# Prompt heads of a decoder step: the values of two heads together, and sums over later key blocks made on GpSimd

## The reference

```python
z = jnp.einsum('bqhd,bkhd->bhqk', q, k) * (SB_HEAD_DIM ** -0.5)
z = z + bias[None, :, None, None]
causal = (k_pos[None, :] < q_pos[:, None])[None, None]
log_stay = jnp.where(causal, jax.nn.log_sigmoid(-z), 0.0)
between = lax.cumsum(log_stay, axis=3, reverse=True) - log_stay
weight = jnp.where(causal, jnp.exp(jax.nn.log_sigmoid(z) + between), 0.0)
return jnp.einsum('bhqk,bkhd->bqhd', weight.astype(v.dtype), v)
```

## Time and profile before

| what | value |
|---|---|
| median of the three runs | 1602.76 us |
| the profiled execution's own time | 1604.15 us |
| its span in the trace | 1602.0 us |
| PE busy, of the span | 1378.6 us (86%) |
| POOL busy, of the span | 236.7 us (15%) |
| stage of the eight heads, from the first scores to the pooling projection | 171.3 to 288.8 us |

### The profile page before, as it was taken

One profiled execution on the slowest core, in us unless ns is written; L12 is line 12 of the kernel. 1 busy time (PEld: TensorE's weight loads), 2 busy tenths in 40 slices (PEclk: granted clock), 3 DMA queues, 4 the chain that ended last, 5 costly groups with the idle time before them and its releaser, 6 DMA issues.

```text
span 1602.0 us, 16163 instructions
## 1 busy us (share of the span) xinstructions
PE 1378.6 (86%) x6201; PEld 1087.4 (68%) x6202; DVE 1004.4 (63%) x1050; ACT 672.6 (42%) x655; POOL 236.7 (15%) x224
## 2 busy tenths in 40 slices
PE   2999799976699999997889999497489999998693
PEld 2785355766588778875768874286478878886582
DVE  3188743234788788863344889613688878882623
ACT  2010443013477777754120025310367777784312
POOL 1042311010122232200000000001103312220000
PEclk7999799995799999997899999697589999999696
DMA  7456445025399999949420220011369999993201
GB/s 278 180 181 277 184 184 184 0 68 198 127 356 369 309 373 368 376 172 331 150 77 1 105 95 15 0 53 55 92 217 377 389 317 382 380 348 122 98 0 54
DMA packets 122741, 314.07 MB, mean 196 GB/s; under 512 B 10060, under 2 KB 10720, under 8 KB 120608
## 3 DMA queue, kind: packets, MB, share of 16 engines
q1 hardware_dynamic: 106350, 249.82, 43.3%
q0 software_dynamic: 14256, 58.69, 10.1%
q10 hardware_dynamic: 2074, 4.71, 1.0%
HBM read 304.17 MB, written 26.70 MB: 207 GB/s over the span
## 4 chain that ended last, share of the span: by engine, by line
PE 72%; DVE 16%; DMA 5%; issue 3%; ACT 3%; SPq 0%; POOL 0%; DVEq 0%; ACTq 0%; POOLq 0%
PE ps L1596 29%; PE ps L1817 10%; PE ps L1818 10%; PE ps L1819 10%; PE ps L1568 3%; DMA ring<-in_w_gate_e 3%; DVE arena L1521 3%; PE ps L1696 2%; DVE rstd L1127 2%; DVE rstd L1135 1%; PE ps L1777 1%; PE ps L1707 1%; DVE xnT L1138 1%; DMA page_of<-in_page_table 1%; PE ps L1585 1%
## 5 line engine op out<-in xcount | busy, mean ns | idle before, releaser
L1596 PE MATMUL ps<-xnT,ring 128*128 128x260 f32 x1920 | 431.1, 388 | 23.1 <-DVE xnT L1138 17.2
L1596 PEld LDWEIGHTS ps<-xnT,ring 128*128 128x128 f32 x1920 | 370.7, 193 | 84.1 <-issue 26.3
L1818 PE MATMUL ps<-ring_parts,arena_parts 128*128 128x512 f32 x768 | 308.2, 401 | 0.0
L1398 DVE TENSOR_TENSOR ring_parts<-ring,xnT_parts 128x2048 fp32r<-128x2048 f32 x96 | 219.2, 2290 | 47.4 <-ACT xnT_parts L941 46.3
L1398 DVE TENSOR_TENSOR ring_parts<-ring,arena_parts 128x2048 fp32r<-128x2048 f32 x96 | 219.7, 2290 | 39.5 <-ACT arena_parts L941 37.9
L941 ACT ACTIVATE xnT_parts<-ring 128x2048 fp32r<-128x2048 f32 x96 | 183.4, 1917 | 85.1 <-PE ps L1819 76.7
L941 ACT ACTIVATE arena_parts<-ring 128x2048 fp32r<-128x2048 f32 x96 | 183.6, 1918 | 77.3 <-PE ps L1819 57.1
L1818 PEld LDWEIGHTS ps<-ring_parts,arena_parts 128*128 128x128 f32 x768 | 148.1, 193 | 32.1
L1817 PE MATMUL ps<-xnT_parts,arena_parts 128*128 128x512 f32 x384 | 158.3, 412 | 10.1 <-DVE arena_parts L1402 10.1
L1817 PE MATMUL ps<-arena_parts 128*128 128x512 f32 x384 | 156.0, 406 | 8.9 <-DVE arena_parts L1402 5.1
L1819 PE MATMUL ps<-xnT_parts,arena_parts 128*128 128x512 f32 x384 | 154.7, 403 | 0.0
(11 more groups left out here) (251 smaller groups left out, 1469.4 us busy)
## 6 DMA issues: line engine op xcount, KB each, us to landing
ring<-in_w_gate_e SPq DMA_DIRECT2D x32, 2048.0 KB, 17.0
ring<-in_w_up_e SPq DMA_DIRECT2D x32, 2048.0 KB, 16.0
ring<-in_w_down_e SPq DMA_DIRECT2D x32, 2048.0 KB, 18.2
ring<-in_w_in_ab SPq DMA_DIRECT2D x4, 2048.0 KB, 26.1
ring<-y_rows SPq DMA_DIRECT2D x16, 512.0 KB, 7.8
ring<-in_w_ple_gate SPq DMA_DIRECT2D x4, 2048.0 KB, 17.7
ring<-in_w_in_c SPq DMA_DIRECT2D x4, 2048.0 KB, 20.8
x_rows<-arena ACTq DMA_DIRECT2D x10, 416.0 KB
```

The source lines that it names most:

```text
L1398: v.tensor_tensor(w_lo, w, high[hu0 % 4].bitcast(F32), ALU.subtract).then_inc(s_lo, 1)
L1596: ins = mm(s[:, half, 0:HALF], w[:, k, :], src[:, k, half * HALF:(half + 1) * HALF], start=(k == 0), stop=(k == n - 1))
L1818: mm(ps[:, bank, :], x, w_lo, start=False, stop=False)
```

## The change

Two edits in the same loop. First, GpSimd now adds up the softplus blocks after masking, in a spare buffer of 640 columns: for each strip kb < 3 one tile holds the sum of all blocks behind it, and `sticks` needs one product with `ones` per strip, three in all where there were six. Second, `values` takes two heads: after the mask of both, it issues the product of head 2p and that of head 2p + 1 for each key block in turn, into the lower and the upper half of bank 6. It is called in the even steps only, in step h for the heads h - 2 and h - 1, and it raises s_pv by 2 at its end.

```diff
+        spare = [xnT[:].rearrange("p k t -> p (k t)")[:, 3360:4000], sq[:].rearrange("p a b -> p (a b)")[:, 0:640]]
...
                 pool.wait_ge(s_sp, h + 1)
-                mask(ex[:, h % 2, :]).then_inc(s_spm, 1)
+                sp, later = ex[:, h % 2, :], spare[h % 2]
+                link(mask(sp))
+                pool.tensor_copy(later[:, 0:P], sp[:, 1024:1024 + P])
+                pool.tensor_copy(later[:, 256:256 + P], sp[:, 512:512 + P])
+                link(pool.tensor_tensor(later[:, P:256], sp[:, 1024 + P:1280], sp[:, 896:1024], ALU.add))
+                pool.tensor_tensor(later[:, 256 + P:640], sp[:, 512 + P:896], later[:, 0:256], ALU.add
+                                   ).then_inc(s_spm, 1)
...
-                sp = ex[:, h % 2, :]
+                sp, later = ex[:, h % 2, :], spare[h % 2]
+                behind = (later[:, 256:640], later[:, 0:256], sp[:, 896:1024])
                 for kb in range(4):
-                    for src in range(kb, 4):
-                        off = (src - kb) * P
-                        width = TP - src * P
-                        ins = mm(ps_flat[:, c0 + at[kb] + off:c0 + at[kb] + off + width],
-                                 tri[:] if src == kb else ones[:], sp[:, at[src]:at[src] + width],
-                                 start=(src == kb), stop=(src == 3), skip_group_check=True)
+                    col, width = c0 + at[kb], TP - kb * P
+                    ins = mm(ps_flat[:, col:col + width], tri[:], sp[:, at[kb]:at[kb] + width],
+                             start=True, stop=(kb == 3), skip_group_check=True)
+                    if kb < 3:
+                        ins = mm(ps_flat[:, col + P:col + width], ones[:], behind[kb],
+                                 start=False, stop=True, skip_group_check=True)
                 ins.then_inc(s_cf, 1)
...
-            def values(h):
-                pe.wait_ge(s_wm, h + 1)
-                if h >= 2 and h % 2 == 0:
-                    pe.wait_ge(s_ot, h // 2)
-                rows = slice(64 * (h % 2), 64 * (h % 2) + 64)
+            def values(p):
+                pe.wait_ge(s_wm, 2 * p + 2)
+                if p:
+                    pe.wait_ge(s_ot, p)
                 for kb in range(4):
-                    ins = mm(ps[rows, 6, kb * P:TP], v_tok[:, kb, h * DH:(h + 1) * DH],
-                             zs3[h % 3][:, at[kb]:at[kb] + TP - kb * P], start=(kb == 0), stop=(kb == 3),
-                             skip_group_check=True)
-                ins.then_inc(s_pv, 1)
+                    for h in (2 * p, 2 * p + 1):
+                        rows = slice(64 * (h % 2), 64 * (h % 2) + 64)
+                        ins = mm(ps[rows, 6, kb * P:TP], v_tok[:, kb, h * DH:(h + 1) * DH],
+                                 zs3[h % 3][:, at[kb]:at[kb] + TP - kb * P], start=(kb == 0), stop=(kb == 3),
+                                 skip_group_check=True)
+                ins.then_inc(s_pv, 2)
...
-                if h:
-                    values(h - 1)
+                if h >= 2 and h % 2 == 0:
+                    values(h // 2 - 1)
                 sticks(h)
...
-            values(SBH - 1)
+            values(SBH // 2 - 1)
```

## The result

The changed kernel takes 1616.84 us (median of 4 runs, 1614.58 to 1620.34), the one before 1602.35 us beside it. The ratio is 1.0094, with a 95% interval of 1.0069 to 1.0120: slower by 11 to 19 us. The direction was forecast, the size was not: +6.0 us was said, and the median lies just above the upper end of the range (1616.0), while that of e9, 1615.61, lies just inside it. The profiled execution took 1617.42 us, 13.3 more than that of before, and its span is 1615.7 us.

The account below looks back on a forecast made before the run. TensorE bounded each head before; afterwards a second chain through DVE, exponential and GpSimd would: 23.6 + 1.3 (GpSimd held) + 1.7 (clock) = 26.6 against 23.81 us per two heads. In all +6.0, 1608.8 us; range 1601.5 to 1616.

Parts of the forecast that it names:

- The path: Odd heads: sample_values, scores, values pair, then L892 to L1249, L1258 to softplus mask, sums, sticks; 23.6 us per two heads.
- the sums on GpSimd: Between softplus mask and sticks: GpSimd's copies and adds, hidden by nothing, take 1.5 us per head (1.2 to 2.1).
- the lower clock over the sticks: Sticks of odd heads: after over 4 us idle, TensorE runs partly at 1.2 GHz, costing 1.7 us (0 to 3.55).
- the stretch up to head 1: Until head 1's sticks end: GpSimd held until 198.95, then sums and slow sticks, ending at 205.7 for 205.28, +0.4 us.
- the +6.0 goes through to the end: Behind the eight heads: a chain through TensorE starts when the stage ends, so the stage's +6.0 us reaches the total.
- L892 (now L899) of head 3 released by the pair of values: Heads 3, 5 and 7: this instruction waits for the values pair behind the scores, so it starts 2.30 us later.
- the values pair: Values on TensorE: two heads run at once in 2.30 us, saving 9.2 us in all.
- GpSimd held for 1.3 us beside L1252: Odd heads: DVE's instruction with two SBUF operands blocks GpSimd's selections and sums for 1.3 us (0 to 1.5).
- the stretch behind head 7: After head 7's sticks: 10.5 us before, the values pair at 2.30 us behind the same mask, so change 0.
- Rival 1: Stage of the heads: TensorE still bounds it, saving 4.1 us in each of three pairs, 12 us, to 1591; 5%.
- the rivals 2 and 3: Second chain binds: without GpSimd's hold and clock loss, 1599, 7%; with clock loss alone 1605 or hold alone 1602, 20% together.
- Rival 4: GpSimd's sums cost 3 us, 1.5 more on each of the four odd heads, giving 1615; 8%.

Follow-up runs that it names:

- e9: The changed kernel run again unaltered, in more runs: median 1615.61 us, ratio 1.0078 to the kernel before.
- e4: The changed kernel with filler products on TensorE between turn_sample and the wait for the sums at heads 3, 5 and 7: ratio 1.0067 to before.
- e11: The changed kernel without DVE's L1252, min(z, -z); ScalarE takes the absolute value instead: ratio 1.0025 to before.
- e1: The kernel before with only the values in pairs; sticks keep ten products and GpSimd makes no sums: ratio 1.0026 to before.
- e5: The changed kernel with a fourth buffer for z and the weights, so L899 waits for the values of head h - 4: ratio 1.0019 to before.
- e10: The kernel before with GpSimd masking the softplus of head h ahead of the weights of head h - 1: ratio 0.9983 to before.
- e6: The changed kernel with a fourth buffer for z and the weights, and GpSimd's softplus mask and sums ahead of the weights' mask: 1595.44 us, ratio 0.9963.
- e7: The changed kernel with values one head at a time, and GpSimd's softplus mask and sums ahead of the weights' mask: ratio 0.9969 to before.
- e3: The changed kernel with only GpSimd's order turned, softplus mask and sums ahead of the weights' mask of the head before: 1603.31 us, ratio 1.0002.

## Why the prediction was right or wrong

**What failed.** The path was right in the stage; the sum over it was not. Three of its terms for the stage were too small: the sums on GpSimd (1.5 us taken, 1.86 measured), the lower clock over the sticks (1.7 taken; 1.9, 2.0 and 2.7 measured) and the stretch up to head 1 (+0.4 taken, +1.3 measured), in which the time that GpSimd's sums hold DVE, 0.7 us, was put at nothing. So the stage grew by 9.2 us where 6.0 were forecast. That alone would have given about 1612 us, well inside the range. The larger part of the miss is the step "the +6.0 goes through to the end": against the stage the median has 5 us more, in e9 4 us more, and the cause of these stays open.

**What held.** That TensorE would cease to bound, and each instruction of the chain that took its place, came out as described: L892 (now L899) of head 3 released by the pair of values (213.35); the values pair 2.33 us (2.30 taken); the sticks at 3.55 us in e4; GpSimd held for 1.3 us beside L1252 (1.3 taken; e11 takes it away); the stretch behind head 7 10.5 us (10.5 taken). Rival 1 fell in the profile after (two heads at 27 us, not 19.7), and e1, which has the pairs without the sums, is no faster either; the rivals 2 and 3 fell with e11 and e4, each of which found one of the two terms at its size or above. Rival 4 was right in direction: dearer sums, by 0.4 us and not 1.5. The Trainium skill's rule on the shared port ("SBUF — State Buffer", section "Who interferes with whom") spoke against this change, and the trace agrees on the size, 2.33 us for 1.03 beside an instruction of 1.49. GpSimd also holds DVE, which the prediction left out: see 3 below. (A slip without weight: the values at 221.37 in the earlier trace rows are those of head 2, not of head 1.)

**The stage: four sizes.** The forecast gave +2.8, +2.8, 0 for the three pairs, +0.4 up to head 1, 0 behind head 7. Measured: +3.25, +3.4, +1.2, +1.3, 0.0, together +9.1 for +6.0. The chain for heads 1 to 3, 3 to 5 and 5 to 7, term by term from the rows above and their like:

| term | forecast | 1 to 3 | 3 to 5 | 5 to 7 |
|---|---|---|---|---|
| sample_values, scores, pair, hand-over | 6.6 | 6.6 | 6.6 | 6.6 |
| L899 to L1265 | 7.1 | 7.0 | 7.0 | 7.0 |
| L1265 to the end of the masks | 4.9 + 1.3 (5 to 7: 4.9) | 6.2 | 6.2 | 4.9 |
| sums | 1.5 | 1.86 | 1.86 | 1.85 |
| sticks at 2.4 GHz, and the clock | 3.55 + 1.7 | 5.4 | 5.6 | 6.3 |
| sum | 26.6, 26.6, 25.3 | 27.1 | 27.2 | 26.6 |

1. The sums were mis-sized: 1.5 taken, 1.86 measured with their waits, inside the bounds of 1.2 and 2.1. The copies took 0.29 where 0.17 to 0.29 had been the bounds, and the last add 0.72 where 0.61 was taken. On three pairs: +1.1 us.
2. The clock was mis-sized: 1.7 taken in all three pairs, 1.9, 2.0 and 2.7 measured: +1.5 us. It was priced from values of 2.30 us, which cannot show more than 2.30 us of loss; the sticks are longer. Head 7 has the longest pause ahead (no scores of a head 8), and its sticks were the slowest, 6.26 us; that the pause's length is the reason is not shown, since in e5 the sticks of head 3 took 6.5 us and those of head 5 took 5.4, each behind 2.73 us idle. e11 is a second case of the spread: its sticks took 5.3, 6.2 and 6.7 us.
3. Up to head 1 one meeting was left out. The prediction had GpSimd held by L1252 until 198.95, the time that L1245 ends in the trace before. But L1252 came 0.86 us later than its twin. 0.2 of it is the later start of the stage; 0.7 is DVE held at head 0 by GpSimd's new sums, in the small adds of the sample tokens (L1233, two SBUF operands), whose last two took 0.38 and 0.78 us where their twins in the trace before took 0.23 each:

```profile
186.03 0.23 DVE arena L1226
...
186.34 0.78 DVE arena L1233
...
186.30 0.72 POOL L701 TENSOR_TENSOR xnT<-arena,xnT 128x256 f32<-128x256 f32 x1
```

The first line is from the kernel before, the others from the changed one. The seven adds of L1233 together take 2.53 us for 1.83, in all nine traced kernels with the sums (2.52 in some), and 1.83 in before, e1 and e10, which have none. The chain of DVE then carries the delay to head 1, where the masks were done at 198.49 and the first copy met L1252:

```profile
198.27 1.56 DVE L1252 SCALAR_TENSOR_TENSOR arena<-xnT 128x1280 f32<-128x1280 f32 x1 [1.91 <-ACT xnT L899]
198.56 1.43 POOL L698 COPY sq<-arena 128x128 f32<-128x128 f32 x1
...
201.59 2.04 PE L1702 MATMUL ps<-arena,tri 128*128 128x512 f32 x2 [6.38 <-POOL sq L701]
```

The copy was held until 199.99, the other sums and their waits took 1.6 us, and the sticks began 1.2 us later than said; they took 5.17 us against 5.25 said. With the first scores 0.2 us later than before, this is +0.9.

**Behind the stage.** The forecast let its +6.0 go through to the end unchanged. The end of the stage is at 298.13 for 288.77, +9.4 with a start 0.2 later. The next mark, the second reciprocal of 128 x 520, is at 354.48 before and here:

```profile
364.83 3.40 DVE L1142 RECIPROCAL rstd<-rms 128x520 f32<-128x520 f32 x1 [2.02 <-ACT rms L862]
```

So +10.4: 66.7 us behind the stage for 65.7, and 66.7 again in e9; but the other kernels have 64.0 to 67.3 there, so this 1.0 is not shown to be the change's. Of the remaining 3 us, 2.8 arose between two later reciprocals, at 1102.08 and 1502.32 before, 400.2 us apart there and 403.1 after. It is 403.8 in e9, but also 403.0 in e10, which has the stage of before, 406.1 in e11, and 398.1 to 402.3 in the others, whatever their stage was. The stretch between these two marks moves as well: 747.6 us before, 748.1 after, but 744.8 in e9 and 741.8 in e4. None of these stretches holds an instruction that the change touches, and they move by some microseconds from one execution to the next. The medians of after and e9 lie 14.5 and 13.1 us above those of the runs of before beside them, and the stage explains 9.2 and 9.4 of that; the intervals begin at 11 and 8 us. In the nine other kernels ratio and stage agree to 3.3 us, with e4, e6, e7 and e10 1.6 to 3.3 us below what the stage says. So about two thirds of the slowdown are explained step by step; whether the other 4 to 5 us are the spread of executions or something of the change behind the stage stays open.

## What to carry to other kernels

When an engine is relieved, look for the ring that runs beside it and write out the whole of it, with the wait that the new order adds, before counting the saving: 12 us of TensorE's work were saved here, and the stage grew by 9, of which 6 went away when a fourth buffer undid the later return of the third. Where an engine serves two chains, put first what the bound engine waits for; here a turned order and a fourth buffer made the same two edits 0.4% faster than before in place of 0.8 to 0.9% slower, though with the sums alone the turned order did not shorten the stage. Try each half of a change by itself: the sums alone, without the pairs, had the stage of the best kernel. And when an engine gets new work, ask whom it will hold as well as who will hold it. Price a pause of TensorE on all the work behind it: in the changed kernel the lower clock lasted some 3.5 us into it, in e3 12 us.

## What the runs showed of the hardware

- GpSimd's short instructions: a copy of 128 x 128 float32 takes 0.29 us, an add of two such 0.45, one of 128 x 256 0.72, and copies behind each other start 0.24 apart. The added 128 columns cost 0.27 us, 2.1 ns each; the Trainium skill ("GPSIMD Engine Reference", section "3.1 Elementwise — side-by-side cycle accounting") has about 2.6 cycles per element, an estimate of 2.2 ns at 1.2 GHz, and the trace agrees. The fixed part, some 0.18 us of each, makes up 0.7 of the 1.86 us of the four.
- Beside a DVE instruction with two SBUF operands of 1.49 us, GpSimd loses 1.1 to 1.3 us whichever of its instructions is caught: the selections (2.33 for 1.03), a copy (1.43 for 0.29), an add (1.86 for 0.72). The other way round, where GpSimd's instruction is the one that runs, DVE waits: an add of 0.23 us issued 0.04 us into a GpSimd add of 0.72 took 0.78 and ended 0.1 us behind it, and L1252 in e5, with the end of a GpSimd add beside it, took 1.68 for 1.49.
- Two products of 64 output rows in the two column halves run beside each other: 16 records in 2.33 us where one head's eight take 2.30.
- turn_sample's small products (8 records, 1 us) did not keep TensorE's clock up: in the changed kernel they ran at 222.57, and the granted clock was 0.76 from 224 and 0.50 from 226 on.
